# Expert pair weights strewn into a zeroed DRAM table by GpSimd's indirect adding transfers, in place of one-hot products on TensorE

## What is computed

```python
q = (hb @ wq).reshape(tc, PEER_HEADS, 2, PEER_HALF)          # 8 heads
s = einsum('thpk,hpnk->thpn', q, keys)                       # 128 keys on each of 2 sides
s_top, i_top = top_k(s, 16)
cand = s_top[:, :, 0, :, None] + s_top[:, :, 1, None, :]
cid = i_top[:, :, 0, :, None] * N_KEYS + i_top[:, :, 1, None, :]
best, pos = top_k(cand, 16)                                  # 16 pairs (i, j) per head
eid = take_along_axis(cid, pos)                              # expert number i * 128 + j
g = softmax(best)
act = gelu(einsum('td,thed->the', hb, u[eid]))
return einsum('the,thed->td', g * act, v[eid])
```

## Time and profile before

| | |
|---|---|
| runs, median | 4057.71 us (4057.68 and 4057.74) |
| the profiled execution, span | 4058.2 us |
| TensorE busy | 3915.4 us, 96% |
| VectorE busy | 3021.8 us, 74% |
| ScalarE busy | 1831.6 us, 45% |
| GpSimd busy | 6.5 us |
| DMA, 16 engines | 752 MB, 185 GB/s, 52.5% of their time |
| TensorE's granted clock | 0.99 of full |

### The profile page before, as it was taken

How to read it: one execution, slowest core, us unless ns; L and a number is a source line. 1 busy time by engine, 2 the same in 40 slices (tenths; PEclk the granted TensorE clock), 3 DMA queues, 4 the chain that set the end, 5 groups by cost and what they waited for, 6 DMA issues and landing times. The chain is left out here.

```text
span 4058.2 us, 66160 instructions
## 1 busy us (share of the span) xinstructions
PE 3915.4 (96%) x25874; PEld 3500.9 (86%) x25874; DVE 3021.8 (74%) x6784; ACT 1831.6 (45%) x2929; POOL 6.5 (0%) x18
## 2 busy tenths in 40 slices
PE   7999999999999999999999899999999799998999
PEld 6768999988889999988887699999888688988798
DVE  4557797788886877788984579777888767766875
ACT  3344444443334444433444344444333535555454
POOL 0000000000000000000000000000000000000000
PEclk8999999999999999999999999999999899999999
DMA  5144575566667865567751357655666422442243
GB/s 218 60 162 152 191 227 176 169 203 239 244 228 271 315 232 169 169 237 254 258 205 57 121 169 232 193 169 182 243 244 244 158 86 91 178 175 104 78 167 146
DMA packets 121829, 752.17 MB, mean 185 GB/s; under 512 B 15728, under 2 KB 17265, under 8 KB 57265
## 3 DMA queue, kind: packets, MB, share of 16 engines
q1 hardware_dynamic: 121520, 747.93, 52.5%
HBM read 693.88 MB, written 54.00 MB: 184 GB/s over the span
## 5 line engine op out<-in xcount | busy, mean ns | idle before, releaser
L1922 DVE TENSOR_TENSOR expert_ring_low<-expert_ring,expert_high 128x1024 fp32r<-128x1024 f32 x768 | 935.6, 1219 | 248.0 <-ACT expert_high L2192 247.7
L2192 ACT ACTIVATE expert_high<-expert_ring 128x1024 fp32r<-128x1024 f32 x768 | 811.8, 1057 | 619.0 <-PE ps L2119 616.0
L2088 PE MATMUL ps<-peer_hT_high_peer,expert_high 128*128 128x256 f32 x3072 | 882.3, 287 | 1.2 <-DVE expert_ring_low L1922 1.0
L2089 PE MATMUL ps<-peer_hT_low,expert_high 128*128 128x256 f32 x3072 | 861.0, 280 | 0.0
L2090 PE MATMUL ps<-peer_hT_high_peer,expert_ring_low 128*128 128x256 f32 x3072 | 861.0, 280 | 0.0
L2088 PEld LDWEIGHTS ps<-peer_hT_high_peer,expert_high 128*128 128x128 f32 x3072 | 583.2, 190 | 3.3 <-DVE expert_ring_low L1922 2.4
L2089 PEld LDWEIGHTS ps<-peer_hT_low,expert_high 128*128 128x128 f32 x3072 | 584.0, 190 | 0.0
L2090 PEld LDWEIGHTS ps<-peer_hT_high_peer,expert_ring_low 128*128 128x128 f32 x3072 | 578.9, 188 | 0.0
L2119 PE MATMUL ps<-expert_high,weighted_high 128*128 128x512 f32 x1536 | 474.9, 390 | 7.4 <-DVE weighted_low L1952 7.4
L2119 PE MATMUL ps<-expert_high,weighted_low 128*128 128x512 f32 x1536 | 473.8, 390 | 0.0
L2119 PE MATMUL ps<-expert_ring_low,weighted_high 128*128 128x512 f32 x1536 | 473.4, 389 | 0.0
(11 more groups left out here) (720 smaller groups left out, 6924.3 us busy)
## 6 DMA issues: line engine op xcount, KB each, us to landing
expert_ring<-in_peer_u SPq DMA_DIRECT2D x192, 1024.0 KB, 5.2
expert_ring<-in_peer_v SPq DMA_DIRECT2D x192, 1024.0 KB, 4.9
gelu_peer<-gelu_out SPq DMA_DIRECT2D x186, 256.0 KB, 5.5
gelu_in_peer<-gelu_peer SPq DMA_DIRECT2D x93, 512.0 KB, 5.7
weight_ring<-in_ffn_w_up SPq DMA_DIRECT2D x22, 2048.0 KB, 7.3
weight_ring<-in_w_in SPq DMA_DIRECT2D x14, 2048.0 KB, 7.4
weight_ring<-in_w_mod SPq DMA_DIRECT2D x12, 2048.0 KB, 8.1
weight_ring<-in_peer_wq SPq DMA_DIRECT2D x12, 2048.0 KB, 7.3
```

Source lines behind the costliest of these rows:

```text
L1922: dve.tensor_tensor(piece(low, n), piece(raw, n), high[:, n % LEAD, :].bitcast(F32), ALU.subtract).then_inc(low_done, 1)
L2088: pe.matmul(o, b[:, s], hT_h[:, c, :], start=(c == 0), stop=False)
L2089: pe.matmul(o, b[:, s], hT_l[:, c, :], start=False, stop=False)
L2192: act.activation(high[:, n % LEAD, :], piece(raw, n), ACT.Identity).then_inc(high_done, 1)
```

## The change

The pair weights of all 256 tokens of a call no longer pass through TensorE:

- three tables in DRAM, one per call, [16384 pairs x 256 tokens] float32, index (i * 128 + j) * 256 + token;
- they are zeroed in the first mixer: `CLEARS` = 12 steps of 2 transfers, each of 2 MB in runs of 512 bytes, from a zero row of SBUF, put by SP between the loads of ring units u0+3, u0+4 and u0+5 (four steps behind each);
- `select()` makes for each tile the shares right after its keys, and the flat positions `spots` (uint32); exponentials are taken per tile;
- GpSimd, for each tile and each of the 128 pairs, issues one indirect transfer that adds 128 shares (one per token) to the table at the 128 positions; after the 16 of a head it waits for them to land, since two heads may pick the same pair;
- then it issues eight loads of 2 MB that bring the table to `wt`; VectorE waits for all eight before V. SP's wait before it reloads `x` is on the strewing. With `TABLED` = `GROUPS` = 0, transposes, one-hots, table products and their copies are gone.

Core of the diff:

```diff
+def clear_pairs(G, sp, n):
+    k, q = divmod(n, CLEARS // CALLS)
+    rows = N_KEYS // (CLEARS // CALLS)
+    dst = pairs_by_key(G, k)[:, q * rows:(q + 1) * rows, :]
+    for t in range(STREWN):
+        sp.dma_start(dst[:, :, t * P:(t + 1) * P], G.zero[:, :].unsqueeze(1).broadcast_to([P, rows, P])).then_inc(G.pairs_cleared, 16)
...
                         sp.dma_start(dst, src).then_inc(S.consts_landed, 16)
+                    for n in range(CLEARS):
+                        ws.run_ahead(sp, u0 + 4 + n // 4)
+                        clear_pairs(G, sp, n)
                     ws.run_ahead(sp, u0 + 6)
...
-GROUPS = W // TOKS
-TABLE_AT = N_KEYS - GROUPS
+STREWN = 2
+TABLED = (PT - STREWN) * P
+GROUPS = TABLED // TOKS
+TABLE_AT = 64
+CALLS = 3
+STREWN_KEYS = 8
...
-                at["shift"] = at["now"]
-                for t in range(PT):
                     dve.wait_ge(exp_ready, t + 1)
...
+                    if t < STREWN:
+                        step(dve.scalar_tensor_tensor(where[:, :], sel[:, t, 0, :], float(N_KEYS), sel[:, t, 1, :], ALU.mult,
+                                                      ALU.add))
...
+                    if t < STREWN:
+                        dve.tensor_scalar(spots[:, t, :], where[:, :], float(STREWN * P), G.rank[:, t:t + 1], ALU.mult,
+                                          ALU.add).then_inc(spots_ready, 1)
...
-            dve.wait_ge(w_out, GROUPS)
+            if GROUPS:
+                dve.wait_ge(w_out, GROUPS)
+            dve.wait_ge(G.pairs_landed, 16 * STREWN_KEYS * (turn_no + 1))
...
+        @block.gpsimd
+        def _(pool):
+            pool.wait_ge(G.pairs_cleared, 16 * CLEARS * STREWN)
+            for t in range(STREWN):
+                pool.wait_ge(spots_ready, 2 * t + 2)
+                for h in range(PEER_HEADS):
+                    for m in range(h * PEER_TOPK, (h + 1) * PEER_TOPK):
+                        pool.indirect_dma_start(pairs, bass.IndirectOffsetOnAxis(spots[:, t, m:m + 1], 0), shares[:, t, m:m + 1],
+                                                None, compute_op=ALU.add).then_inc(G.strewn, 16)
+                    pool.wait_ge(G.strewn, 16 * ((turn_no * STREWN + t) * PAIRS + (h + 1) * PEER_TOPK))
+            if TABLED:
+                pool.wait_ge(table_ready, PT - STREWN)
+            if mod is not None:
+                pool.wait_ge(mod_out, 1)
+            rows = N_KEYS // STREWN_KEYS
+            for q in range(STREWN_KEYS):
+                pool.dma_start(wt[:, q * rows:(q + 1) * rows, 0:STREWN * P],
+                               pairs_of[:, q * rows:(q + 1) * rows, :]).then_inc(G.pairs_landed, 16)
...
-            sp.wait_ge(w_ready, W)
+            if TABLED:
+                sp.wait_ge(w_ready, TABLED)
+            sp.wait_ge(G.strewn, 16 * (turn_no + 1) * STREWN * PAIRS)
```

More of the change, by code:

```diff
@@ L55 @@
 SCOPES = []
-STAGE_SEMS = 30
-BIG_SEMS = 89
+STAGE_SEMS = 29
+BIG_SEMS = 88
 @contextmanager
@@ L1785, in peer_experts @@
         mod.slots = arena.take("mod_slots", [P, 2, UNIT], F32)
-    table, hot_i, hot_j, ge_in, aw, ah, al = small
+    spots, shares, table, hot_i, hot_j, ge_in, aw, ah, al = small
     if end.cols:
@@ L1801, in peer_experts @@
     G.e_turn += 1
+    pairs, pairs_of = G.pairs[turn_no], pairs_by_key(G, turn_no)
+    where = arena.take("spot_sums", [P, PAIRS], F32)
     N = 2 * N_KEYS
@@ L1832, in expert, with group_at @@
             return (p + N_KEYS - KEPT) % N_KEYS
+        def group_at(r):
+            g, odd = divmod(r - TABLE_AT, STREWN + 1)
+            return g if odd == 0 and 0 <= g < GROUPS else None
         def mod_unit(r):
@@ L1865, in select @@
                                       ALU.subtract).then_inc(shift_ready, 1)
+                    at[f"shift{t}"] = at["now"]
                     pflat = pos[:, :, :].rearrange("p h m -> p (h m)")
@@ L1910, in select @@
+                    dve.tensor_tensor(share.rearrange("p (h m) -> p h m", h=PEER_HEADS), ex[:, t, :, :],
+                                      sm[:, t, :, 1:2].broadcast_to([P, PEER_HEADS, 16]), ALU.mult).then_inc(
+                                          spots_ready if t < STREWN else sel_ready, 1)
                     yield 300
-                for t in range(PT):
+                for t in range(STREWN, PT):
                     at[f"turn{t}"] = at["now"] + TURN_AFTER
                     yield (TURN_AFTER + 1) * SELECT_NS
-                    dve.wait_ge(sel_turned, t + 1)
-                    dve.tensor_copy(table[:, :, t * P:(t + 1) * P],
-                                    ps[:, 3, 0:3 * P].rearrange("p (k c) -> p k c", k=3)).then_inc(table_ready, 1)
+                    dve.wait_ge(sel_turned, t - STREWN + 1)
+                    o = (t - STREWN) * P
+                    dve.tensor_copy(table[:, :, o:o + P], ps[:, 3, 0:3 * P].rearrange("p (k c) -> p k c", k=3)).then_inc(table_ready, 1)
@@ L2025, in _ @@
                         at["late"] = r
-                if r >= TABLE_AT - 1 and r - TABLE_AT + 1 < GROUPS:
-                    hots(r - TABLE_AT + 1)
-            dve.wait_ge(w_out, GROUPS)
+                if group_at(r + 1) is not None:
+                    hots(group_at(r + 1))
+            if GROUPS:
+                dve.wait_ge(w_out, GROUPS)
+            dve.wait_ge(G.pairs_landed, 16 * STREWN_KEYS * (turn_no + 1))
             for r in range(2):
@@ L2154, in _ @@
                         mod.sums(pe, u, parts_out, sums_ready)
-                if r >= TABLE_AT:
-                    table_of(r - TABLE_AT)
+                if group_at(r) is not None:
+                    table_of(group_at(r))
+            if mod is not None and not GROUPS:
+                pe.wait_ge(mod_out, 1)
             def turn_front(q):
@@ L2212, in _ @@
                 gelu(r)
-                if r == N_KEYS - 1:
+                if r == N_KEYS - 1 and group_at(r) is not None:
                     table_out(GROUPS - 2)
@@ L2216, in _ @@
                 split_high(r + LEAD)
-                if r == at["shift"]:
-                    for t in range(PT):
+                for t in range(PT):
+                    if r == at[f"shift{t}"]:
                         act.wait_ge(shift_ready, t + 1)
@@ L2225, in _ @@
                         mod.out(act, sums_ready, mod_out)
-                if TABLE_AT < r < N_KEYS - 1:
-                    table_out(r - TABLE_AT - 1)
+                if group_at(r - 1) is not None and (r < N_KEYS - 1 or group_at(r) is None):
+                    table_out(group_at(r - 1))
             def std(k):
@@ L2752, in peer @@
         mine = Arena(nc, own, 2 * D * 4)
-        table = mine.take("pair_table", [P, 3, W], F32)
+        spots = mine.take("pair_spots", [P, STREWN, PAIRS], U32)
+        shares = mine.take("pair_shares", [P, STREWN, PAIRS], F32)
+        table = mine.take("pair_table", [P, 3, max(TABLED, P)], F32)
         hot_i = mine.take("hot_i", [P, TOKS, P], F32)
@@ L2794, in peer @@
         ws.limit = None
-        peer_experts(nc, G, hs, (pq, keysT), scores, later, dead, wt, (table, hot_i, hot_j, ge_in, aw, ah, G.w_low), src_u, src_v, ge_dram,
+        peer_experts(nc, G, hs, (pq, keysT), scores, later, dead, wt, (spots, shares, table, hot_i, hot_j, ge_in, aw, ah, G.w_low), src_u, src_v, ge_dram,
                      [(G.x[:, ts, :], G.x_spill[:, ts, :])], mod, end)
@@ L5089, in make_shared @@
     G.e_turn = 0
+    G.pairs = [nc.dram_tensor(f"pair_weights_{k}", [N_KEYS * N_KEYS * STREWN * P, 1], F32).ap() for k in range(CALLS)]
+    G.pairs_cleared = nc.alloc_semaphore("pairs_cleared")
+    G.strewn = nc.alloc_semaphore("shares_strewn")
+    G.pairs_landed = nc.alloc_semaphore("pairs_landed")
     G.moved = nc.alloc_semaphore("rows_moved")
```

40 lines of the change are left out of this document (25 added, 15 removed).

## The result

The changed kernel takes 4929.01 us (median; 4928.26 and 4929.76) where the kernel before takes 4057.71: a ratio of 1.2144, 95% interval 1.2109 to 1.2179. Slower was the likelier side, but 871 us more is far beyond the forecast of 333 and above the range's end of 4750.

A forecast was written before the change was run, and what follows sets the result against it. TensorE, busy 96% of the span, was taken to bound the kernel. With V 236 us later over three calls and clears costing 97: 4058 + 236 + 97 = 4391 us, range 3930 to 4750; slower 0.65.

The forecast's parts named there:

- (a), the strewing: GpSimd's indirect transfers before V in each call: 389 us (bounds 150 and 614), ending at +474, +486, +474.
- the middle, 1.4 us: Price assumed per indirect transfer issued by GpSimd, between 0.47 us bare issue and 2.4 us one at a time.
- Locked out: Rival: VectorE's two-input splits block GpSimd in U rows, up to 120 us per call, 4751 us; chance 0.2 with engines bound.
- The 16 waits for a head's landing: GpSimd's waits in each call's strewing for a head's transfers to land: 16 x 1.9 us.
- The bounds, 0.47 and 2.4 us: Price per indirect transfer from below (SP's plain issue spacing) and from above (one at a time, landing included).
- The products go: U rows without table products: 68 us less per call, 204 in three; rows end at +367, +401, +367.
- (b) The load: 16.8 MB of weights loaded behind the strewing, nothing else running: 47 us, V at +521, +533, +521.
- The few us of lower clock: TensorE, at rest before V, restarts at its lower clock: a few us, not counted in the sum.
- The clearing: Zeroing stores in the first mixer delay mask and modulation units behind them: +97 us at 200 GB/s, bounds 0 and +180.
- Strewn in time: Rival: GpSimd spends under 0.8 us per transfer, V starts near +400 or earlier; 3857 to 4050 us, chance 0.27.
- The DMA engines become the bound: Rival: 0.1 us per 4-byte add makes U loads some 95 us late; 4391 + 0 to + 200, chance 0.2 with lock-out.
- The signs: Expected in the profile: U rows at 2.87 us, TensorE idle some 150 us before V, transfers 1.4 us apart, late u0+5 and mask.

The follow-up runs named there:

- experiment 1: Changed kernel with VectorE's split of each U row cut to 128 of its 1024 columns, and products reading only those; 4759.3 us.
- experiment 9: Changed kernel, both tiles strewn, with VectorE's split of each U row from row 64 on cut into four instructions of 256 columns; 4799.5 us.
- experiment 3: Changed kernel with the indirect transfers writing in place of adding; 4479.7 us.
- experiment 4: Changed kernel with 64 in place of 128 addresses in each indirect transfer; 4689.1 us.
- experiment 8: Changed kernel with one tile strewn, the other by one-hots, and VectorE's split in four instructions from row 64 on; 4107.9 us, ratio 1.0118.
- experiment 12: As experiment 11, with VectorE's split in rows 32 to 63 run as two instructions of 512 columns; 4034.2 us, ratio 0.9927 to the kernel before.
- experiment 5: Changed kernel with only the first head's shares strewn, 32 transfers per call in place of 256; 3948.7 us, 0.97 of the kernel before.
- experiment 11: Changed kernel with one tile strewn, V waiting for the weights by parts, the other tile's one-hots two rows ahead; 4028.5 us, ratio 0.9925 to the kernel before.
- experiment 7: Changed kernel with one tile strewn and the other by one-hot products in every second row from row 64, tables half the size; 4091.2 us.

## Why the prediction was wrong

**The step that failed is (a), the strewing**, by its size: "the middle, 1.4 us" per transfer, with VectorE's lock left out of it. It forecast 389 us of strewing. From the first transfer to the load's first issue call 1 took 587 us. Counted with the measured pieces:

- A transfer that nothing disturbs: 1.55 us and 0.30 us to the next, 1.85 us and not 1.4. 256 x 0.45 = 115 us.
- Held by VectorE: the 103 transfers of the U rows are together 67 us longer than alone. "Locked out" was right as a mechanism, but the prediction priced it as another case, with a chance of its own, where it comes *on top of* the forecast. Its "up to 120 us" supposed that GpSimd loses all of the split's 43%; a transfer is held once at most, up to 0.97 us by a split, and not at all when it begins first. Calls 2 and 3 have 64 and 69 us: 200 us in three calls, not 360. Experiments 1 and 9 show the cause: shorten or cut the split, and the holds of call 1 fall from 67 us to under 4 and to 20.
- The 16 waits for a head's landing: 41 us in place of 30. Some 5 us of that are in the 1.85 already, so 6 us more than forecast. Behind the U rows they are as forecast, in them longer; in call 2 the waits behind a head are 13 us more than in call 1.
- Five pauses of 1.9 to 3.0 us inside heads, behind the first 60, 113, 120, 180 and 226 transfers of the call, in which GpSimd waits for nothing that the profile shows: 10 us that the prediction did not have. Calls 2 and 3 have them at the same places, experiments 3 and 4 only behind 113 and 226. Their cause is open.

115 + 67 + 6 + 10 = 198 us, which is the 587 less the 389. The bounds, 0.47 and 2.4 us, were right, and so was the reason for not taking the lower end. The middle had no row behind it; the range of (a) alone reached 614 us, which would have given V at +746 and holds the +718.5 measured. The range of the whole stopped short of it at 1.8 us per transfer, and the lock was never added to a slow transfer. So 1.85 us and the lock together lie outside every case of the prediction. In three calls V is late by 841 us in place of 236: 605 us too little. Against this the clears were taken 79 us too dear (18 for 97), so the miss of 538 us would have been larger still with the clears right.

The Trainium skill (SBUF — State Buffer, "SBUF: two separate sides") says that a VectorE instruction with two SBUF inputs holds GpSimd's reads of SBUF until it ends. The timeline (a transfer begins 0.13 us after the split and is 0.97 us longer than alone) and experiment 9 agree, for a transfer whose addresses lie in SBUF. What experiments 8 and 12 show beside it, a transfer held through several instructions that follow each other, stays without a cause. The other page cited, DMA: Bandwidth & Descriptors, "Anatomy of one DMA", gives a fixed 2.0 us for a transfer issued from GpSimd, from setup to completion. Here the last transfer of a head takes 1.55 us and the next starts 1.7 to 1.9 us after it behind the U rows, 3.2 to 3.5 us together: the measurement is longer, and its first part, the 1.55 us which bound this kernel, is what the forecast lacked.

**The products go**: right. The U rows are 367.2, 397.0 and 367.1 us long for +367, +401, +367. In call 2 the estimate was 4 us high.

**(b) The load**: right, 44 us for 47. That nothing runs beside it holds too. The few us of lower clock, "not counted", are seen: granted 0.50 while TensorE rests and in the first 4 us of V, 0.93 on the mean in the 6 us behind them.

**The clearing**: the size was wrong, +97 for 15 to 18 us at the first U product. 512-byte runs were expected at 200 GB/s; eight stores of 2 MB with a unit's load go at some 300 GB/s. By SP's timeline u0+4 is issued at 122.95 (before: 91.40), u0+5 at 186.80 and the mask at 249.78, when 248.1 is its due time. The mechanism was right: a queue that holds back what stands behind the clears. But the longest wait is not the mask's: ScalarE waits 7.0 us for u0+5, which was to be used at 194.7, VectorE 4.3 us for the mask and TensorE 1.9 us for a modulation unit. Below are SP's timeline and the first of these waits (us in all, times, longest).

```profile
68.81 54.10 SPq L1562 DMA_DIRECT2D pair_weights<-zero_row  x8
122.95 7.25 SPq L172 DMA_DIRECT2D weight_ring<-in_ab_w_in  x1
130.24 56.52 SPq L1562 DMA_DIRECT2D pair_weights<-zero_row  x8
186.80 7.22 SPq L172 DMA_DIRECT2D weight_ring<-in_ab_w_in  x1
194.07 55.59 SPq L1562 DMA_DIRECT2D pair_weights<-zero_row  x8
249.78 7.39 SPq L1713 DMA_DIRECT2D scan_mask<-in_scan_mask  x1
...
ACT pieces_high L717 <- DMA weight_ring<-in_ab_w_in: 7.0, 1, 7.0
```

**"Strewn in time"** decided from 1.1 us and is out; experiment 5 shows what it would have been worth, 2.7%, not the 5% at its best end, since the load slows the U rows by 25 us when it runs in them. **"The DMA engines become the bound"** supposed 0.1 us per add. Behind the U rows the share is 0.24 with 154 transfers of 128 addresses, 8 for each of the 16 engines: 0.24 x 304.1 / (154 x 8) = 0.06 us of an engine for each. The engines stand at 0.77 in the U rows, which keep their length. It is out as well, for adding transfers; experiment 3 shows that its other half, U loads late and TensorE starved, does happen with plain ones, and at engines far from busy.

**The signs**: an idle TensorE, ended by a transfer into the expert weights, came as named, but for 352 us and not 150; unit u0+5 and the mask were late as named; the U rows kept their length. The spacing of 1.4 us and the last transfers at +474, +486, +474 were the signs that failed.

Sum with the measured terms: 4058 + 841 + 18 + 9 = 4926, the span.

## What to carry to other kernels

Count the issue of an indirect transfer as work of GpSimd, here 1.86 us each whatever the DMA engines do, and multiply it before anything else: 256 of them are longer than the 68 us of TensorE that they replace by seven times. Moving work to an idle engine moves it to that engine's price, and its idle time beside VectorE is not free: two-input instructions of VectorE hold GpSimd's transfers. When two mechanisms can act at once, add their prices in the forecast; do not set them against each other as rivals. Where GpSimd must run beside such a loop, it can help to cut VectorE's long instructions into pieces (experiment 9; in 8 and 12 it won nothing), to start what consumes the result on its first part, and to split the work between the engines so that neither ends last (experiment 11).

## What the runs showed of the hardware that was not expected

- GpSimd's transfers fall in step with VectorE's splits: one per U row, 2.83 us apart, each begun 0.13 us after a split and held by it for 0.97 us. A transfer shorter by 0.14 us isn't caught in this and goes 1.88 us apart on the mean, a third less.
- Which VectorE instruction runs when a transfer begins decides. The splits and selection's two-input instructions hold it. One-input reductions, maxima and index searches do not: in call 1 of the changed kernel a transfer begun with 1.61 us of a reduction still to run took 1.56 us. A one-hot (one input) does at times: in version 11 transfers begun 0.14 us after one took 1.63 us, and in version 7 three, with a split following within 0.12 us, took 2.7 to 2.8 us.

```profile
611.47 2.28 DVE L1930 TENSOR_REDUCE selected<-one_hot 128x128 f32<-128x2048 f32 x1
612.14 1.56 POOL L2328 DMA_INDIRECT pair_weights<-pair_shares,pair_spots  x1 [0.30 <-issue]
```

- Plain indirect writes of 4 bytes, 1.26 us apart, brought all transfers together down to 83 GB/s at a DMA share of 0.27, and the U rows went from 367 to 548 us; with the add, 1.86 or 2.83 us apart, the U rows kept their length. The profile's row of GpSimd's queue gives 114048 packets with the add and 28032 without, a difference of 112 for each of the 768 transfers. The cause stays open.
- The reverse: two one-input instructions of VectorE (one-hots) that ran 0.4 to 0.7 us after a transfer's start took 0.65 and 0.46 us in place of 0.34 and 0.28; the others beside it kept their length (experiment 7).
- With rows of half the length in the table (experiment 7), GpSimd sat 35 us between the seventh and the eighth of the load's parts. With both tiles it issued all eight in 4 us.
- The clears hold SP itself: eight stores of 2 MB keep it 54 to 57 us, and each later issue takes 7 us.
